# Where the sums of squares stand at the borders of the first two mixers, and one weight split ahead of two additions

## The reference

```
h = rms_norm(x, norm_mix[l])
z = h @ w_in[l]                     # attention, convolution and recurrence inputs
... attention, short convolution, gated recurrence (sigmoids of a part of z)
x = x + y @ w_out[l]
x = x + ffn(rms_norm(x, norm_ffn[l]))   # dense SwiGLU in layer 0, 8 experts in layer 1
```

## Time and profile before

| | |
|---|---|
| median of 3 runs | 2555.1 us (2554.83 to 2555.97) |
| the profiled execution | 2549.77 us, of which the span is 2548.0 us |
| TensorE matmuls busy | 2498.7 us, 98% |
| VectorE busy | 1885.1 us, 74% |
| ScalarE busy | 1495.8 us, 59% |
| mean granted TensorE clock | 0.996 |

### The profile page before, as it was taken

The page is one execution under the profiler, slowest core; times in us unless marked ns, Lnnn a source line. Parts: engine busy times, 40 slices in busy tenths (PEclk is TensorE's granted clock), DMA queues, the critical chain, the costliest instruction groups (busy, mean ns, idle before and its releaser), DMA issues.

```text
span 2548.0 us, 38641 instructions
## 1 busy us (share of the span) xinstructions
PE 2498.7 (98%) x16734; PEld 2231.6 (88%) x16734; DVE 1885.1 (74%) x1665; ACT 1495.8 (59%) x1520; POOL 0.2 (0%) x4
## 2 busy tenths in 40 slices
PE   9999999999999999999999999999999999999998
PEld 8889999877888888888888887998899999899998
DVE  7765556858888888888888888657775575777655
ACT  6463336457777777777777777446553455565433
POOL 0000000000000000000000000000000000000000
PEclk9999999999999999999999999999999999999999
DMA  6335554325999999999999998433345553243552
GB/s 247 133 116 183 182 183 148 133 84 190 364 358 362 359 363 355 363 349 367 352 364 357 364 356 313 173 132 116 133 166 188 178 180 133 101 162 122 188 190 83
DMA packets 83520, 585.38 MB, mean 230 GB/s; under 512 B 9420, under 2 KB 11308, under 8 KB 12820
## 3 DMA queue, kind: packets, MB, share of 16 engines
q1 hardware_dynamic: 83348, 582.87, 61.8%
HBM read 581.79 MB, written 1.05 MB: 229 GB/s over the span
## 4 chain that ended last, share of the span: by engine, by line
PE 88%; DVE 7%; ACT 3%; issue 1%; DMA 0%; DVEq 0%; ACTq 0%
PE PS L1798 87%; DVE wlo L1053 2%; ACT whi L555 1%; PE PS L2331 1%; PE PS L2012 1%; ACT pb L667 1%; DVE stat L1200 1%; DVE pb L1214 1%; DVE hT L1099 0%; ACT pt L684 0%; DVE xT L1378 0%; DVE hlo L1105 0%; DVE pb L1218 0%; DVE hlo L1069 0%; DMA raw<-in_ws 0%
## 5 line engine op out<-in xcount | busy, mean ns | idle before, releaser
L1053 DVE TENSOR_TENSOR wlo<-raw,whi 128x2048 fp32r<-128x2048 f32 x550 | 1257.9, 2290 | 361.7 <-ACT whi L555 352.9
L555 ACT ACTIVATE whi<-raw 128x2048 fp32r<-128x2048 f32 x550 | 1052.0, 1914 | 310.3 <-PE PS L1798 273.4
L1798 PE MATMUL PS<-hhi,whi 128*128 128x256 f32 x1984 | 573.1, 289 | 10.0 <-DVE hlo L1105 2.6
L1798 PE MATMUL PS<-hlo,whi 128*128 128x256 f32 x1984 | 562.4, 283 | 0.0
L1798 PE MATMUL PS<-hhi,wlo 128*128 128x256 f32 x1984 | 562.2, 283 | 0.0
L1798 PEld LDWEIGHTS PS<-hhi,whi 128*128 128x128 f32 x1984 | 381.3, 192 | 24.5 <-issue 16.3
L1798 PEld LDWEIGHTS PS<-hlo,whi 128*128 128x128 f32 x1984 | 381.4, 192 | 0.7 <-issue 0.5
L1798 PEld LDWEIGHTS PS<-hhi,wlo 128*128 128x128 f32 x1984 | 381.3, 192 | 0.0
L1798 PE MATMUL PS<-whi,xghi 128*128 128x512 f32 x896 | 359.9, 402 | 1.2 <-DVE wlo L1053 1.1
L1798 PE MATMUL PS<-whi,xglo 128*128 128x512 f32 x896 | 355.0, 396 | 0.0
L1798 PE MATMUL PS<-wlo,xghi 128*128 128x512 f32 x896 | 354.9, 396 | 0.0
(11 more groups left out here) (374 smaller groups left out, 3574.8 us busy)
## 6 DMA issues: line engine op xcount, KB each, us to landing
raw<-in_wm SPq DMA_DIRECT2D x336, 1024.0 KB, 5.6
raw<-in_ws SPq DMA_DIRECT2D x214, 1024.0 KB, 4.8
xT<-in_xT SPq DMA_DIRECT2D x4, 256.0 KB, 6.8
bsum<-in_bsum SPq DMA_DIRECT2D x1, 1024.0 KB
out_T<-hT SPq DMA_DIRECT2D x4, 256.0 KB, 2.5
lmask<-in_lmask SPq DMA_DIRECT2D x1, 512.0 KB
onehot_in<-in_onehot SPq DMA_DIRECT2D x1, 288.0 KB
lbw<-in_lbw SPq DMA_DIRECT2D x1, 256.0 KB
```

Source lines behind the costliest of these rows:

```text
L555: act.activation(whi[s % SPLIT][:], raw[s % RAW][:], ACT.Copy).then_inc(hi_ready, 1)
L1053: dve.tensor_tensor(wlo[s % SPLIT][:], raw[s % RAW][:], whi[s % SPLIT][:].bitcast(F32), ALU.subtract).then_inc(lo_ready, 1)
L1798: return pe.matmul(out, a, b, start=start, stop=stop, skip_group_check=True)
```

## The change

Two edits. In `sums_to_x` the split of the mixer's second unit is put ahead of presum(2) for every i, which alters only the call with i = 2, at the border into layer 1's first mixer. In `first_units` the norm sums with columns are put within unit 2, after its 24th matmul, as those without columns are; this alters both first mixers. No instruction is added or removed.

```diff
@@ sums_to_x (DVE)
                 if i != 8:
-                    if i == 6:
-                        split_lo(used - 1 + LEAD)
+                    split_lo(used - 1 + LEAD)
                     presum(2)
                     presum(3)
                     presum_out()
-                    if i != 6:
-                        split_lo(used - 1 + LEAD)
@@ first_units (TensorE)
                 unit1(bank1, uhi[l], ulo[l], True)
                 empty(bank1, 1, freed1)
-                if columns:
-                    norm_sums(True)
-                    unit2(bank2, uhi[l], ulo[l])
-                else:
-                    unit2(bank2, uhi[l], ulo[l], between=lambda f, k: (f, k) == (0, DK - 1) and norm_sums())
+                unit2(bank2, uhi[l], ulo[l], between=lambda f, k: (f, k) == (0, DK - 1) and norm_sums(columns))
                 empty(bank2, 1, freed2)
```

## The result

| | before | after |
|---|---|---|
| median | 2554.39 us (20 runs, 2549.30 to 2557.53) | 2558.68 us (20 runs, 2557.00 to 2562.12) |
| ratio to before, 95% interval | | 1.0023 (1.0016 to 1.0029) |
| profiled execution | 2549.77 us | 2558.75 us |
| its span, granted clock | 2548.0 us, 0.996 | 2557.0 us, 0.994 |

The change is slower. By the ratio it is 5.9 us, between 4.1 and 7.4; the forecast was 6.6. (Before was measured again beside the changed kernel, hence the 2554.39 beside the 2555.1 known at the prediction.)

What follows compares the result with a forecast made beforehand. The chain from the sums of squares through ACT and DVE to unit 4 was taken to bind where the edits act. Terms 3.99 + 2.63 = +6.6 us on 2555.1 gave 2561.7 us, with an 8-in-10 range of 2557.5 to 2564.

Steps and rivals of the forecast that it cites:

- The binding chain: Both first mixers: from the sums of squares to unit 4, what follows the sums on ACT and DVE sets the end.
- Term 1: Layer 0's start: sums go behind unit 2's 24th matmul, so rcol and unit 4 come 3.99 us later.
- Term 2: Layer 1's border: with both edits, the first sigmoid and unit 4 come 2.63 us later.
- the old wait for DVE: Layer 1's border: before, DVE's two wlo held the first sigmoid 0.2 us; after the change they are no longer last.
- The cover of 0.3 us for wlo in (a): Layer 1's border: unit 2's wlo is done at 416.44, before unit 1 ends at 416.74; unit 2 starts 1.55 us earlier.
- The unknown cost: Both borders: sums with columns amid a unit, not shown by the trace; 0.97 us from sums to rcol was taken.
- neither bound: From the sums' start to rcol: 0.93 us at the least, 1.7 with unit 2 matmuls let in between.
- the table load: ACT's sigmoid table at layer 1: trace shows 1.28 us, skill page about 2.66, making term 2 an estimated 1.38 larger.
- Nothing is given back: Rival, behind unit 4: TensorE's waits in each first mixer return 1.3 us, leaving +4.0, 2559.1 us; chance 0.13.
- TensorE did not decide: Rival: TensorE, not the chain, decides; -0.7 us at layer 1, nothing at the start, 2554.4 us; chance 0.04.
- The start is not spared: Rival: nothing changes at layer 0's start as unit 2 is late anyway; only term 2 stands, 2557.7 us; chance 0.05.
- The clock rival: Clock falls in new idle time ahead of unit 3: +0.3 us at one border, at worst +1.6 at each; chance 0.10.

Runs made afterwards that it cites:

- its two parts alone: Against the kernel before: second edit only in layer 0's first mixer, ratio 1.0023; both edits only at layer 1's border, ratio 1.0012.
- the kernel with ones in both waits: Kernel before plus second block's sums earlier, fourth unit's whi moved on ACT, seven unread constant matmuls in each of two first-mixer attention waits (n = 3, 4): ratio 0.9961.

## Why the prediction was right

**The binding chain** was read rightly: it starts at the sums. 6.55 us from the sums to unit 3, wherever they stood, is the plainest evidence. **Term 1** was 3.99 and is 3.99: the sums at 22.22 less the 0.18 of start-up, rcol 0.97 us behind them as at the other border, unit 4 at 35.67 less 0.18. **Term 2** was 2.63 and is 2.61, by its own steps: rcol was to be 2.85 later and is 2.83 (5.33 behind L591's load instead of 2.50), of which the 0.2 of the old wait for DVE come off. The cover of 0.3 us for wlo in (a) held, as unit 2 has no wait, and the sums stand 8.55 us behind unit 1's first matmul (417.50 to 426.05), as taken from the second mixer. **The unknown cost**, sums with columns amid a unit, is 0.97 to rcol (22.05 to 23.02), the value taken; neither bound was needed.

**On the table load** the Trainium skill ("ScalarE: Activation LUTs", What ACT_TABLE_LOAD costs) has 2.66 us, which would have put the sigmoids an estimated 1.38 later; the load at 428.34 is followed by the sigmoid at 429.64, 1.30 behind it. The row was right to decide.

**The rivals.** Nothing is given back: every ACT instruction from 450 us to the experts is 9.1 us later, within 0.07. TensorE did not decide: unit 3 waited 2.67 and 2.66 us for hlo. The start is not spared: it has 3.99 of the 6.6. The clock rival did come about, and cheaply, as its price said: in the changed kernel's profile the clock fell right in unit 3 of layer 1,
```profile
432.00:436.00 4.00, 3.40 (x17) 3.44 (x18) 3.90 (x8) 2.21 (x5) 0.00 (x0) 0.62 0.01 2
```
and the keys behind unit 4 were still only 2.63 late (445.91 against 436.82, less the 6.46 that stood before the border): unit 3's spare time took nearly all of it. What the prediction missed about the clock is its place. It looked at the new idle times, while the old ones in the attention decide up to 3 us a mixer from one execution to the next; unit 4 was expected at 437.3 from the span's start and came at 439.91, as 2.64 us of low clock in the attention lie ahead of it. The runs don't show that the change caused them: its two parts alone had 0.5 and 1.4 us, and the kernels with the first mixers' sums where they were had from 0 to 2.6. Nor do they rule it out.

**The medians.** The forecast's 2561.7 was carried by a before of 2555.1 from three runs; 20 runs have it at 2554.39, with 8 of them from 2549.30 to 2551.27 and 12 from 2554.20 to 2557.53. The measured 2558.68 lies inside the range of 2557.5 to 2564, but under the forecast's own 2560.2 to 2563.5 and nearest to the rival that gives part back (2559.1); it is the timeline of ACT that decides for the forecast. The 5.33 us from the profiled execution to the median were carried over as they stood: after the change the median is 0.07 under the profiled execution. So two terms that are right within 0.02 us go with a median that is 3 us off. The ratio, 1.0023 against 1.0026 forecast, is the better witness than the difference of the medians, 4.3 us, but its interval, 4.1 to 7.4 us, alone would not tell 6.6 from 4.3.

## What to carry to other kernels

Ask of each small reduction whether its result heads the chain on other engines: if the chain of waits leaves TensorE at it, then ahead of the next unit is its place, and "hiding" it amid the unit costs what the unit's first part lasts, here 0.119 us a matmul, and with it the unit's wait for its own weights. A pattern that stands elsewhere in the kernel is no witness that it is free: in the second block, where it had stood all along, it kept TensorE 1.31 us idle. A place where such a sum heads no chain, and the move would cost nothing, was not among these. And an engine's short waits between dependent steps (1.03 us on ACT here) are where its independent work paid, more than ahead of or behind the whole sequence.

## What the hardware showed unexpectedly

With the same work and 8.35 of 12 us busy in the attention's end in both profiles, before and then after,
```profile
132.00:144.00 12.00, 8.35 (x78) 7.29 (x78) 7.95 (x20) 9.48 (x25) 0.00 (x0) 1.00 0.01 1
```
```profile
132.00:144.00 12.00, 8.35 (x73) 5.97 (x71) 8.59 (x22) 9.37 (x29) 0.00 (x0) 0.95 0.00 0
```
the granted clock behind it was 1.00 in one and 0.77 in the other, 2.64 us apart. (The changed kernel's work stands 3.82 us later; the stretch moved by as much, 135.82 to 147.82, has 8.35 busy too, at a clock of 0.79.) In the kernel with ones in both waits, 11.58 of the 12 us were busy and the clock was 1.00. What decides it from one execution to the next no run here shows. Matmuls whose results nobody reads, put into waits, cost 0.04 and 0.05 us in the two first mixers of that profile; with seven of them on a busy TensorE the mixer took 1.56 us more.
